# Sliding-window softmax of a hybrid decoder layer: 256 keys selected into 128 columns, parted again by GpSimd

## The chip, the cores and the metric

The kernel runs on one core of a Trainium2 chip. The metric is the device time of one execution in microseconds. The engines are TensorE (PE in the profile; PEld are its weight loads), VectorE (DVE), ScalarE (ACT), GpSimd (POOL) and SyncE (SP), which issues nearly all DMAs.

## The reference

One layer on x of 2048 tokens by 1024 channels. A projection gives the inputs of two groups of heads; group A is a gated DeltaNet (4 heads of 128), group B a sliding-window softmax (8 query heads of 64, 2 key heads). Their outputs are gated, joined, projected, added to x and normalised. The change is in group B:

```python
WINDOW = 128
BLOCK = 128
    dist = q_idx + BLOCK - s_idx                       # q_idx 0..127, s_idx 0..255
    mask = ((dist >= 0) & (dist < WINDOW))[None] & (key_pos >= 0)[:, None, :]
    s = s - slopes[:, :, None, None, None] * dist.astype(jnp.float32)
    s = jnp.where(mask, s, -jnp.inf)
    m = jnp.maximum(jnp.max(s, axis=-1), sink)
    p = jnp.exp(s - m[..., None])
    p = p / (jnp.sum(p, axis=-1, keepdims=True) + jnp.exp(sink - m)[..., None])
    o = jnp.einsum('bhgnqs,bnshd->bnqhgd', p.astype(vb.dtype), vb)
```

A block of 128 queries looks at 256 keys, its own block and the one before. The mask leaves exactly 128 of the 256 open for each query: in column j it is the key of the own block if j is at most the query's row, otherwise the key of the block before.

## The kernel before

The 2048 tokens are four units of 512; a unit has four slots, one for each pair of heads (n = 0 to 15), and a slot does one head of group A and one pair of query heads of group B over the 512 tokens. Between the steps of the heads TensorE does the dense work (the projections of the slots to come, L849, and the output projection of finished tiles, L900): `JOBS` lists it in order, each job with a begin and an end in slots, and `fill_to(n, f)` issues what is due up to the share f of slot n. `Places` holds the shares at which the steps of the heads stand. Every engine has its own program in fixed order, written out in `slot(n)`; `after(engine, counter, n, k)` makes an engine wait for a semaphore.

Group B works in two halves of 256 tokens (e = 0 and 1), each with two blocks (cc) and two heads (hd). For one half:

- TensorE `scores(n, e)` (L957) writes 256 key columns for each block and head into banks 2 and 3.
- VectorE `maxima` (L1752) adds the bias (ALiBi slope times distance, with masked keys far down), stores to `score` and takes the row maximum. ScalarE `weights` (L1353) takes the exponential with its row sum. VectorE `divide` (L1774) multiplies by the inverse of the sum.
- TensorE `turns(n, e)` (L972) transposes each 128 by 128 square of `score` into banks 2 and 3; ScalarE `copy_turned` (L1367) copies back, one bank each time.
- TensorE `values(n, e)` (L990) multiplies with `v_ring`; VectorE `gate_b` (L1782) multiplies with the gate into `y_out`, and SP spills that (`spill_b`, L668).

Between them stands group A's work: the base inverses of 16 by 16 blocks (`base_inverses`, L1793 to L1805, a chain of 30 small VectorE instructions and two closing ones, ending in `t_ready`, for which TensorE waits at L1067), further steps of the inverse (L1073 to L1095), and then the recurrence over four chunks: state product (L1107), residual (VectorE L1915), L1117, v_new (L1919), L1120, state (L1922). In the first half the transposes stand at about a quarter of the slot, ahead of the base inverses' end, and the values right before L1067; in the second half the transposes stand shortly before the recurrence and the values right before its first chunk. The convolutions (`convs`, L1582, with the small copies L1586 and L1589) are VectorE work placed between.

GpSimd subtracts the rounded part of the weights from the raw weights (`lows`, L783, four instructions for each tile): tiles of w_in in slots -1 to 2, of w_out in slots 3 and 4, and two pieces of x in slots 7 and 11. Near the end it scales and shifts output tiles 8 to 10 (L813, L817), each when VectorE has normalised it. In slot 15, SP's list is: loads of y (9 to 13), `store_tile(8)`, `load_x_tile(10)` into the buffer that tile 8 leaves, `load_y(14)`, `store_tile(9)`, and so on. VectorE's `add_half` (L1638) waits for the tile of x.

## Time and profile before

| | us |
|---|---|
| median of 3 runs | 1089.53 |
| lowest, highest | 1089.48, 1092.77 |
| the profiled execution, its own time | 1090.27 |
| its span in the trace | 1088.5 |
| VectorE busy | 688.7 |
| ScalarE busy | 532.7 |
| GpSimd busy | 115.9 |

The span runs from the first to the last instruction of the trace. Busy times of a pipelined TensorE overlap: what a group costs is better read from start to start. A row of a group gives line, engine, operation, tiles, shape and count, then busy time and mean duration, then the idle time before it. TensorE's granted clock was 0.999 of full speed.

### The profile page before, as it was taken

What the parts mean: (1) busy time and instruction counts of PE and PEld (TensorE: products, weight loads), DVE (VectorE), ACT (ScalarE), POOL (GpSimd) and SP (SyncE); (2) the same over time, 40 slices, a digit from 0 to 9 for tenths busy, and PEclk for the clock granted to TensorE, in tenths of its full rate; (3) what the DMA queues carried; (4) which work ended last, traced back from release to release, by engine and by line L of the source; (5) the groups of instructions that cost most, each with busy time, mean ns of one, the idle gap of its engine ahead of it and who ended that gap; (6) DMA issues with size and microseconds to landing.
All of it is one profiled execution on the core that took longest, in us unless ns stands there. A gap on an engine that the chain in (4) does not pass through costs nothing.

```text
span 1088.5 us, 19513 instructions
## 1 busy us (share of the span) xinstructions
PE 1064.2 (98%) x7212; PEld 846.5 (78%) x7212; DVE 688.7 (63%) x2081; ACT 532.7 (49%) x1557; POOL 115.9 (11%) x152
## 2 busy tenths in 40 slices
PE   7999999999999999999999999999999999999997
PEld 5877787778778787777887878787787878787885
DVE  5285959584665747576365665757537575758565
ACT  4557675754636454363354535435344555564300
POOL 3413132134100000020000000002000000002210
PEclk9999999999999999999999999999999999999999
DMA  8967475665553626253562551715454343622432
GB/s 282 315 209 262 163 274 195 243 208 183 201 205 109 237 73 235 87 185 98 175 228 93 165 215 46 265 49 185 132 179 157 126 157 128 215 73 63 137 116 77
DMA packets 58430, 183.55 MB, mean 169 GB/s; under 512 B 8480, under 2 KB 21216, under 8 KB 45024
## 3 DMA queue, kind: packets, MB, share of 16 engines
q1 hardware_dynamic: 58192, 182.05, 48.7%
q8 instruction: 57, 0.93, 0.3%
q10 hardware_dynamic: 144, 0.26, 0.1%
q14 instruction: 37, 0.30, 0.1%
HBM read 138.22 MB, written 44.07 MB: 167 GB/s over the span
## 4 chain that ended last, share of the span: by engine, by line
PE 65%; DVE 6%; DMA 2%; issue 1%; ACT 0%; SPq 0%; DVEq 0%
PE bank L849 33%; PE bank L900 10%; PE bank L1137 4%; PE bank L957 2%; PE bank L990 2%; PE bank L972 2%; PE bank L1107 1%; PE bank L1120 1%; PE bank L1117 1%; PE bank L1121 1%; DVE y_cols L1797 1%; DVE y_step L1793 1%; PE bank L1030 1%; PE bank L1045 1%; PE bank L1115 1%
## 5 line engine op out<-in xcount | busy, mean ns | idle before, releaser
L849 PE MATMUL bank<-xr,w 128*128 128x512 f32 x2496 | 653.9, 405 | 7.4 <-DVE xr L1534 7.4
L849 PEld LDWEIGHTS bank<-xr,w 128*128 128x128 f32 x2496 | 449.8, 189 | 101.7 <-issue 9.8
L900 PE MATMUL bank<-wo,y_split 128*128 128x512 f32 x432 | 114.4, 404 | 0.0
L900 PEld LDWEIGHTS bank<-wo,y_split 128*128 128x128 f32 x432 | 77.0, 189 | 14.6 <-issue 0.7
L1582 DVE SCALAR_TENSOR_TENSOR kq<-conv_in,convw_all,kq 128x512 f32<-128x512 f32 x96 | 77.3, 806 | 7.8 <-ACT conv_in L1191 5.8
L1487 ACT ACTIVATE o_scaled<-bank 128x128 f32<-128x128 f32 x64 | 17.7, 277 | 124.5 <-PE bank L1121 124.3
L1353 ACT ACTIVATE score<-score,neg_max 128x256 f32<-128x256 f32 (+1 forms) x128 | 62.7, 493 | 29.0 <-DVE neg_max L1759 29.0
L1919 DVE TENSOR_SCALAR steps<-bank,nb_rk 128x128 f32<-128x128 f32 x64 | 22.3, 348 | 63.9 <-PE bank L1117 63.9
L1922 DVE SCALAR_TENSOR_TENSOR state<-state,cols_all,bank 128x128 f32<-128x128 f32 x64 | 22.2, 347 | 63.2 <-PE bank L1120 63.2
L1793 DVE TENSOR_TENSOR y_step<-blocks,y_cols 128x60 f32<-128x60 f32 (+14 forms) x240 | 50.3, 210 | 12.1 <-DMA blocks<-n_spill 3.3
L783 POOL TENSOR_TENSOR xr<-y_tile,xr 128x256 fp32r<-128x256 f32 x8 | 6.0, 774 | 455.1 <-ACT xr L1172 455.1
L783 POOL TENSOR_TENSOR w<-y_tile,w 128x256 fp32r<-128x256 f32 x48 | 40.1, 866 | 101.0 <-ACT w L1180 62.5
L1797 DVE TENSOR_TENSOR y_cols<-y_step,y_cols 128x56 f32<-128x56 f32 (+6 forms) x224 | 44.4, 198 | 7.7
L1752 DVE CUSTOM_DVE_ANT_0 score<-bank,bias 128x256 f32<-128x256 f32 (+1 forms) x128 | 45.5, 411 | 6.0 <-PE bank L957 5.7
L1915 DVE SCALAR_TENSOR_TENSOR steps<-bank,cols_all,v_tok 128x128 f32<-128x128 f32 x64 | 22.1, 346 | 42.5 <-PE bank L1107 42.5
L1367 ACT ACTIVATE score<-bank 128x512 f32<-128x512 f32 (+1 forms) x64 | 33.9, 585 | 26.1 <-PE bank L972 26.1
L1137 PE MATMUL bank<-wo,xr 128*128 128x512 f32 x192 | 44.3, 390 | 0.2 <-DVE x_tile L1638 0.2
L1774 DVE TENSOR_SCALAR score<-score,denom_inv 128x256 f32<-128x256 f32 (+1 forms) x128 | 43.1, 400 | 1.1
L1137 PEld LDWEIGHTS bank<-wo,xr 128*128 128x128 f32 x192 | 35.9, 188 | 8.0 <-DVE x_tile L1638 0.6
L1446 ACT ACTIVATE blocks<-bank 128x128 f32<-128x128 f32 x16 | 4.4, 278 | 76.1 <-DVE blocks L1884 76.1
L900 PE MATMUL bank<-wo,w 128*128 128x512 f32 x144 | 38.0, 404 | 0.8 <-DVE w L1722 0.8
L1582 DVE SCALAR_TENSOR_TENSOR v_ch<-conv_in,convw_all,v_ch 128x512 f32<-128x512 f32 x48 | 37.2, 774 | 1.1
(217 smaller groups left out, 1628.3 us busy)
## 6 DMA issues: line engine op xcount, KB each, us to landing
w<-w_split SPq DMA_DIRECT2D x78, 1024.0 KB, 5.4
w_split<-w SPq DMA_DIRECT2D x26, 1024.0 KB, 5.1
blocks<-n_spill SPq DMA_DIRECT2D x32, 256.0 KB
y_spill<-y_out SPq DMA_DIRECT2D x30, 256.0 KB, 5.8
x_tile<-w_in SPq DMA_DIRECT2D x13, 512.0 KB, 6.1
y_tile<-w_in SPq DMA_DIRECT2D x12, 512.0 KB, 6.4
y_tile<-y_spill SPq DMA_DIRECT2D x12, 512.0 KB, 6.1
x_tile<-x SPq DMA_DIRECT2D x12, 512.0 KB, 3.9
```

The costliest lines, as they stand in the source:

```text
L783: ins = nc.gpsimd.tensor_tensor(dst[:, part], raw[:, part], hi[:, part], ALU.subtract)
L849: ins = nc.tensor.matmul(bank[JOBS[at].bank][:], w[:, turn % 3, wp, k, :], xr[:, xp, k], start=(step == 0), stop=(step == 3 * KT - 1))
L900: ins = nc.tensor.matmul(bank[JOBS[at].bank][:], y_place(t)[:, yp, k], wo[:, k, wp, half * UNIT:(half + 1) * UNIT], start=(step == 0), sto ...
L1137: ins = nc.tensor.matmul(bank[JOBS[at].bank][:], xr[:, yp, k, tok * P:(tok + 1) * P], wo[:, k, wp, half * UNIT:(half + 1) * UNIT], start=( ...
L1353: nc.scalar.activation(sc, sc, ACT.Exp, bias=neg_max[:, cc, hd:hd + 1], accum_out=row_sum[:, cc, hd:hd + 1]).then_inc(exp_ready.sem, 1)
L1367: nc.scalar.activation(pick(p_turned(cc)), pick(tiles(bank[2 + cc])), ACT.Copy)\
L1582: ins = nc.vector.scalar_tensor_tensor(acc, conv_in[:, c, step:step + UNIT], convw_all[:, i, c, step:step + 1], acc, ALU.mult, ALU.add)
L1752: nc.vector.tensor_tensor_reduce(out=score[:, cc, hd, 0:keys], in0=bank[2 + hd][:, cc * 256:cc * 256 + keys], in1=bias[:, hd, 2 * P - keys ...
L1774: nc.vector.tensor_scalar(p, p, denom_inv[:, cc, hd:hd + 1], None, ALU.mult).then_inc(p_scaled.sem, 1)
L1793: nc.vector.tensor_tensor(y_step[:, :, rest], blocks[:, j, :, j + 1:], y_cols[:, :, j:j + 1].to_broadcast(wide), ALU.mult).then_inc(base_s ...
L1797: nc.vector.tensor_tensor(y_cols[:, :, rest], y_step[:, :, rest], start, ALU.add).then_inc(base_step.sem, 1)
L1919: nc.vector.tensor_scalar(v_new, bank[6][:, 0:P], nb_rk[:, one], None, ALU.mult).then_inc(v_new_ready.sem, 1)
```

## The change

Before the maxima, VectorE now selects in the banks: with the mask `recent` (distance of the own block's key masked) the past key's score replaces the own one, so that 128 columns hold the 128 open keys. Maxima, exponentials and divisions work on 128 columns (`p_own`). Four squares of 128 by 128 are transposed for each half, into bank 2 alone, and one ScalarE instruction copies them into `p_past`. GpSimd then parts them with two masks: `p_past` times `tri` gives the own block's weights in `p_own`, times `past` the past block's, in place; `values` waits for each block's pair of products. The values of the second half and their gate move into the first chunk of the recurrence. On GpSimd the program becomes one list in the order of the slots, with the splits of weights and x between the parts and the scaling of tiles 8 to 10 behind the last part. On VectorE three set-up instructions are added; from slot 4 on the bias is 128 wide.

```diff
@@ block.gpsimd
+            def part(n, e):
+                if (n, e) == (0, 0):
+                    pool.wait_ge(part_masks, 1)
+                after(pool, p_copied, n, e + 1)
+                for cc in range(2):
+                    for dst, keep in ((p_own, tri), (p_past, past)):
+                        ins = nc.gpsimd.tensor_tensor(dst[:, cc], p_past[:, cc],
+                                                      keep[:].unsqueeze(1).to_broadcast([P, 2, P]), ALU.mult)
+                    ins.then_inc(p_parted.sem, 1)
...
+            turns = [turn for turn in range(TILES_W) if w_by_pool(turn)]
+            while turns[0] < 9:
+                w_low(turns.pop(0))
+            for n in range(SLOTS):
+                s, i = divmod(n, AH)
+                if n < AH - 1:
+                    w_low(turns.pop(0))
+                    part(n, 0)
+                    w_low(turns.pop(0))
+                    part(n, 1)
+                    for turn in turns[0:2]:
+                        w_low(turns.pop(0))
+                elif n == AH - 1:
+                    for ks in ((0, 1), (2, 3)):
+                        for k in ks:
+                            wo_low(k)
+                        part(n, ks[0] // 2)
+                    for k in range(4, KT - 1):
+                        wo_low(k)
+                else:
+                    if n == AH:
+                        wo_low(KT - 1)
+                    if i == AH - 1 and s < SBS - 1:
+                        x_low(s + 1, 2)
+                        x_low(s + 1, 3)
+                    part(n, 0)
+                    part(n, 1)
+            for t in POOL_TILES:
+                scale_tile(t)
@@ block.tensor
             def turns(n, e):
-                s, i = divmod(n, AH)
-                if e == 1 and i == AH - 1 and s < SBS - 1:
-                    after(pe, ba_summed, s + 1, 1)
                 for cc in range(2):
                     after(pe, p_scaled, n, 4 * e + 2 * cc + 2)
-                    if cc == 0:
-                        after(pe, p_scaled, n, 4 * e + 4)
                     for hd in range(2):
-                        for kb in range(1 if (s, e, cc) == (0, 0, 0) else 2):
-                            q = 2 * hd + kb
-                            ins = nc.tensor.transpose(bank[2 + cc][:, q * P:(q + 1) * P],
-                                                      score[:, cc, hd, kb * P:(kb + 1) * P], ident[:])
-                    ins.then_inc(p_turn_done.sem, 1)
+                        q = 2 * cc + hd
+                        ins = nc.tensor.transpose(bank[2][:, q * P:(q + 1) * P], p_own[:, cc, hd], ident[:])
+                ins.then_inc(p_turn_done.sem, 1)
...
             def values(n, e):
-                after(pe, p_turned_ready, n, 2 * e + 2)
...
-                    kbs = (0, 1) if token > 0 else (0,)
+                    kbs = (0, 1) if token > 0 else (1,)
+                    after(pe, p_parted, n, 2 * e + cc + 1)
...
-                values(n, 1)
...
                     nc.tensor.matmul(bank[6][:, 0:P], y_inv[:, c], resid, start=True, stop=True).then_inc(tr_done.sem, 1)
                     fill_to(n, at.chunk(c, 2 / 3))
+                    if c == 0:
+                        values(n, 1)
                     after(pe, v_new_ready, n, c + 1)
@@ block.scalar
             def copy_turned(n, e):
-                for cc in range(2):
-                    after(act, p_turn_done, n, 2 * e + cc + 1)
...
+                after(act, p_turn_done, n, e + 1)
+                nc.scalar.activation(p_past, bank[2][:].rearrange("p (c h n) -> p c h n", c=2, h=2), ACT.Copy)\
+                    .then_inc(p_copied.sem, 1)
@@ block.vector
+            nc.vector.tensor_scalar(past[:], tri[:], -1.0, 1.0, ALU.mult, ALU.add).then_inc(part_masks, 1)
+            nc.vector.tensor_scalar(recent[:], dist[:, P:2 * P], MASKED / 2, None, ALU.is_ge)
+            nc.vector.tensor_tensor(dist[:, 0:P], dist[:, 0:P], dist[:, P:2 * P], ALU.max).then_inc(dist_ready, 1)
...
             def maxima(n, e):
+                lead = (s, e) == (0, 0)
+                for hd in range(2):
+                    both = bank[2 + hd][:].rearrange("p (c k n) -> p c k n", c=2, k=2)[:, int(lead):]
+                    nc.vector.copy_predicated(both[:, :, 0], recent[:].unsqueeze(1).to_broadcast([P, 2 - int(lead), P]),
+                                              both[:, :, 1]).then_inc(packed.sem, 1)
+                after(dve, packed, n, 2 * e + 2)
...
                 for c in range(CH):
                     one = slice(c, c + 1)
-                    if c == 0:
-                        gate_b(n, 1)
...
                     nc.vector.scalar_tensor_tensor(state[:, i], state[:, i], col(EGT)[:, one], bank[4][:, P:2 * P],
                                                    ALU.mult, ALU.add).then_inc(state_ready.sem, 1)
+                    if c == 0:
+                        gate_b(n, 1)
```

## Rows read from the trace of the kernel before

**Rows 1.** The page: its first line and the first engine's busy time.
```profile
span 1088.5 us, 19513 instructions
...
PE 1064.2 (98%) x7212; PEld 846.5 (78%) x7212; DVE 688.7 (63%) x2081; ACT 532.7 (49%) x1557; POOL 115.9 (11%) x152
```

**Rows 2.** Waits of TensorE: who waited for whom, total us, times, longest.
```profile
PE bank L1067 <- DVE steps L1805: 3.8, 6, 1.0
```

**Rows 3.** Timeline of TensorE, slot 7: start, length, engine, line, operation, count.
```profile
485.61 1.04 PE L972 MATMUL bank<-ident,score 128*128 128x128 f32 x8
486.40 0.71 PE L900 MATMUL bank<-wo,y_split 128*128 128x512 f32 x2
```

**Rows 4.** Groups of VectorE by shape: busy us, mean ns, idle before.
```profile
L1752 DVE CUSTOM_DVE_ANT_0 score<-bank,bias 128x256 f32<-128x256 f32 x120 | 43.8, 419 | 5.9 <-PE bank L957 5.7
L1774 DVE TENSOR_SCALAR score<-score,denom_inv 128x256 f32<-128x256 f32 x120 | 41.5, 407 | 1.0
...
L1875 DVE COPY_PREDICATED r<-lower,bank 128x128 f32<-128x128 uint8 x16 | 4.8, 299 | 19.6 <-PE bank L1067 19.6
```

**Rows 5.** Timeline of GpSimd and VectorE in slot 3, beside the base inverses.
```profile
226.27 2.83 POOL L783 TENSOR_TENSOR wo<-y_tile,wo 128x256 fp32r<-128x256 f32 x4 [27.04 <-ACT wo L1186]
...
225.21 0.21 DVE L1793 TENSOR_TENSOR y_step<-blocks,y_cols 128x60 f32<-128x60 f32 x1
...
226.46 0.63 DVE L1797 TENSOR_TENSOR y_cols<-y_step,y_cols 128x52 f32<-128x52 f32 x1
...
235.93 0.31 DVE L1805 STREAM_TRANSPOSE steps<-y 128x128 f32<-128x128 f32 x1
```

**Rows 6.** Timeline of slot 5: the base inverses' first and last instruction, and L1067.
```profile
357.50 0.21 DVE L1793 TENSOR_TENSOR y_step<-blocks,y_cols 128x60 f32<-128x60 f32 x1
...
364.69 0.31 DVE L1805 STREAM_TRANSPOSE steps<-y 128x128 f32<-128x128 f32 x1
...
366.06 0.45 PE L1067 MATMUL bank<-steps,n_t 32*32 32x32 f32 x32
```

**Rows 7.** Timeline of slot 5 from the second transposes to the first chunk.
```profile
376.40 1.04 PE L972 MATMUL bank<-ident,score 128*128 128x128 f32 x8
...
379.13 1.09 PE L990 MATMUL bank<-score,v_ring 128*64 128x128 f32 x16
380.16 0.49 PE L1107 MATMUL bank<-state,kq 128*128 128x128 f32 x2
...
382.09 0.39 PE L1117 MATMUL bank<-steps,y_inv 128*128 128x128 f32 x2
...
383.71 0.38 PE L1120 MATMUL bank<-steps,k_dec 128*128 128x128 f32 x2
...
377.04 1.09 ACT L1367 ACTIVATE score<-bank 128x512 f32<-128x512 f32 x2 [1.42 <-PE bank L972]
...
377.84 2.32 DVE L1582 SCALAR_TENSOR_TENSOR v_ch<-conv_in,convw_all,v_ch 128x512 f32<-128x512 f32 x3
...
380.69 0.34 DVE L1915 SCALAR_TENSOR_TENSOR steps<-bank,cols_all,v_tok 128x128 f32<-128x128 f32 x1
```

**Rows 8.** Timeline of VectorE in slot 0: three convolution steps beside GpSimd.
```profile
66.33 3.04 DVE L1582 SCALAR_TENSOR_TENSOR kq<-conv_in,convw_all,kq 128x512 f32<-128x512 f32 x3
```

**Rows 9.** Line 1617's own instructions: duration min/median/max ns, first and last start.
```profile
L1617 DVE SCALAR_TENSOR_TENSOR pre<-pre,ea x4: 110/111/509, 31.4 to 784.1; 128x16 f32<-128x16 f32 x4
```

**Rows 10.** Timeline of slot 15: GpSimd, SP, VectorE and TensorE around output tile 8.
```profile
999.52 2.82 POOL L813 TENSOR_TENSOR x_tile<-x_tile,gain 128x256 f32<-128x256 f32 x4 [241.55 <-DVE x_tile L1662]
1002.29 2.98 POOL L817 TENSOR_TENSOR x_tile<-x_tile,shift 128x256 f32<-128x256 f32 x4
...
1008.13 0.46 SPq L658 DMA_DIRECT2D out<-x_tile  x1
...
1018.52 0.69 DVE L1638 SCALAR_TENSOR_TENSOR x_tile<-x_tile,bank 128x512 f32<-128x512 f32 x1 [0.59 <-DMA x_tile<-x]
...
1007.01 1.03 PE L972 MATMUL bank<-ident,score 128*128 128x128 f32 x8
```

More of the change, by code:

```diff
@@ L485, in build_layer @@
         denom_step = counter("denom_step", 4)
+        part_masks = sem("part_masks")
+        dist_ready = sem("dist_ready")
+        packed = counter("packed", 4)
         p_scaled = counter("p_scaled", 8)
-        p_turn_done = counter("p_turn_done", 4)
-        p_turned_ready = counter("p_turned_ready", 4)
+        p_turn_done = counter("p_turn_done", 2)
+        p_copied = counter("p_copied", 2)
+        p_parted = counter("p_parted", 4)
         pv_done = counter("pv_done", 2)
@@ L796, in w_low, with wo_low, scale_tile @@
                 lows(flat(1), raw_stage[turn % 2], flat(0)).then_inc(w_ready, 1)
-            for turn in range(TILES_W):
-                if w_by_pool(turn):
-                    w_low(turn)
-            for k in range(KT):
+            def wo_low(k):
                 pool.wait_ge(wo_high, k + 1)
                 lows(wo[:, k, 1], raw_stage[k % 2], wo[:, k, 0]).then_inc(wo_split, 1)
-            for u in (2, 3):
-                x_low(u, 2)
-                x_low(u, 3)
-            for t in POOL_TILES:
+            def part(n, e):
[7 more added lines that the diff above has]
+                    ins.then_inc(p_parted.sem, 1)
+            def scale_tile(t):
                 res = x_bufs[x_buffer(t)[0]]
@@ L881, in sum_g @@
                 after(pe, g_ready, u, 1)
-                if u > 0:
-                    after(pe, p_turned_ready, JOBS[at].n, 4)
                 g = pre[:, 5].rearrange("p h t -> p (h t)")
@@ L935, in scores @@
                     after(pe, kb_copied, s, 1)
-                    after(pe, p_turned_ready, n - 1, 4)
+                    after(pe, p_copied, n - 1, 2)
                     if i == 0:
@@ L940, in scores @@
                 else:
-                    after(pe, p_turned_ready, n, 2)
+                    after(pe, p_copied, n, 1)
                 for cc in range(2):
@@ L1034, in slot @@
                     after(pe, vb_copied, s, 1)
-                    after(pe, p_turned_ready, n - 1, 4)
+                    after(pe, p_copied, n - 1, 2)
                     for c in range(CH):
@@ L1347, in weights @@
                 for cc in parts:
-                    keys = n_keys(n // AH, 2 * e + cc)
                     if cc == 0:
@@ L1351, in weights @@
                     for hd in range(2):
-                        sc = score[:, cc, hd, 0:keys]
+                        sc = p_own[:, cc, hd]
                         nc.scalar.activation(sc, sc, ACT.Exp, bias=neg_max[:, cc, hd:hd + 1],
@@ L1563, in slopes @@
             def slopes(n):
+                width = 2 * P if n < AH else P
                 for hd in range(2):
-                    nc.vector.tensor_scalar(bias[:, hd], dist[:], pair_all[:, n % AH, SLOPE, hd:hd + 1], None, ALU.mult)\
+                    nc.vector.tensor_scalar(bias[:, hd, 0:width], dist[:, 0:width], pair_all[:, n % AH, SLOPE, hd:hd + 1], None, ALU.mult)\
                         .then_inc(bias_ready.sem, 1)
+            dve.wait_ge(dist_ready, 1)
             slopes(0)
@@ L1748, in maxima @@
                     after(dve, pv_done, n, 1)
+                lead = (s, e) == (0, 0)
[4 more added lines that the diff above has]
+                after(dve, packed, n, 2 * e + 2)
                 for cc in range(2):
-                    keys = n_keys(s, 2 * e + cc)
+                    first = P if lead and cc == 0 else 0
                     for hd in range(2):
-                        nc.vector.tensor_tensor_reduce(out=score[:, cc, hd, 0:keys],
-                                                       in0=bank[2 + hd][:, cc * 256:cc * 256 + keys],
-                                                       in1=bias[:, hd, 2 * P - keys:], scale=BD ** -0.5, scalar=LOWEST,
+                        nc.vector.tensor_tensor_reduce(out=p_own[:, cc, hd],
+                                                       in0=bank[2 + hd][:, cc * 256:cc * 256 + P],
+                                                       in1=bias[:, hd, first:first + P], scale=BD ** -0.5, scalar=LOWEST,
                                                        op0=ALU.add, op1=ALU.max, accum_out=row_max[:, cc, hd:hd + 1])\
```

22 lines of the change are left out of this document (8 added, 14 removed).

## The prediction

> **What bounds the kernel now.** I read the page first: TensorE is busy for 1064.2 of the 1088.5 us span [rows 1]. The engine's waits come next: behind the start, the largest is 3.8 us in 6 waits at L1067, for the end of VectorE's base inverses (L1805) [rows 2]. So the time is the sum of what TensorE is given, and any new wait of more than a few tenths of a microsecond is paid in full. The profiled execution took 1090.27 us, 1.77 more than its span and 0.74 more than the median of the runs; the sum below is made against 1090.27 and 0.74 is taken off at the end.
>
> **Fewer transposes.** 248 transposes become 128. Eight of them took 0.79 us from their first start to the start of the matmul behind them [rows 3], 0.1 us each (the 273 ns that one lasts overlaps its neighbour). 120 x 0.1 = 12.0 us less for TensorE, 0.4 us in each of the 32 half slots (0.2 in the first).
>
> **VectorE and ScalarE.** A maximum over 256 keys took 419 ns and a division 407 ns (mean) [rows 4]; both go to 128. The added selection (256 elements, bank to bank) has no row; the nearest is the 128-element copy_predicated at 299 ns [rows 4]. Bounds: 0.3 us (as that one) to 0.9 us (twice it and some) for each; I take 0.4. Two are added per half slot, 0.8 us and 0.1 for the wait behind them, against 4 x 0.13 from the maxima and 4 x 0.03 from the divisions: +0.25 us in VectorE's chain. In slots 3 to 15 it is hidden, since VectorE waits there for TensorE's transposes or inverse steps; in slots 0 to 2 the second half is VectorE's chain down to the division, so 3 x 0.2 = +0.6 us (without cover in all slots it would be 32 x 0.25 = 8). One eviction of 512 columns replaces two, the exponentials halve, the bias is half as wide from slot 4 on: nothing waits for them. The three set-up instructions stand in VectorE's slack before slot 0: nothing.
>
> **GpSimd, first halves.** Each half slot now has four GpSimd products of 256 elements. The same kind on that engine is 2.83 us for four [rows 5], so 3.0 us with the wake-up: 95 us more for an engine that was busy for a tenth of the span. Values of the first half are due about 8 us after the copy, so they do not wait. What pays is VectorE. In slot 3 eight such instructions (the four shown and four more 3.9 us later) ran beside the base inverses; the chain took 235.93 + 0.31 - 225.21 = 11.03 us [rows 5]. With none beside it, it took 364.69 + 0.31 - 357.50 = 7.50 us [rows 6]. That is 3.53 / 8 = 0.44 us for each GpSimd instruction: one small VectorE instruction is held at 0.63 instead of 0.21 us until it ends [rows 5]. The new products follow the first transposes, which is where this chain runs: four fall into it in nearly every slot, +1.76 us.
> - Slots 0, 1, 2, 3, 7 and 11 have no slack at L1067 (TensorE waits there already; in 0 to 2, 7 and 11 the products queue behind a split and still land in the chain): 6 x 1.75 = 10.5, and 0.9 in slot 3, where the next split of w_out slides into the longer chain. 11.4 us.
> - Slots 5, 6, 9 and 10: the chain ended at 365.00 and TensorE came at 366.06 [rows 6], slack 1.06. 1.76 - 1.06 = +0.7 us; four times, 2.8 us.
> - The others, read in the same way: 0 in 4 and 12 (the chain starts late there, on a DMA), -0.4 in 8, +0.3 in 13 and 14, +0.9 in 15. 1.1 us.
> First halves: +15.3 us, the saving of 0.4 included.
>
> **GpSimd, second halves.** The second values move behind the first trial residual. In slot 5 the transposes started at 376.40, the copy at 377.04, and k_dec x v_new (L1120) at 383.71 [rows 7]. GpSimd would run from 377.7 to about 382, values are wanted at about 382.3: hardly a direct wait. But VectorE is then in the convolution of v (377.84, three steps of 0.75) and two small copies, and its residual (L1915) started at 380.69 [rows 7]. Three steps beside GpSimd took 3.04 instead of 2.32 us [rows 8]: +0.7. The copies have no row beside GpSimd. Bounds: nothing, and 1.1 us for both (held to the end of a product each). The nearest row, a small instruction with two SBUF inputs, went from 111 to 509 ns [rows 9]; I take 0.3 each, 0.6. The gate's 0.4 us have moved away, so the residual is ready 0.9 us later than now, at 381.9. TensorE comes for it 1.4 us earlier (0.4 of transposes gone, and the values, 379.13 to 380.16, not yet issued), waits, and issues L1117 at 382.0, where it stood at 382.09; the 1.0 us of values, which hid VectorE's work before, now come after it. L1120 is 0.9 us later than before instead of 0.4 earlier. By slots: 4, 5, 8 and 9 +0.9 each (3.6); 6 and 10, where the residual addition of an output tile stands in the same place and L1117 waits already, +1.9 each (3.8); 12 to 14, with half the filling, +1.0 each (3.0); 0 to 2 +0.9 each and the 0.2 above (3.3); 3, where the second part queues behind a split of w_out, +0.6; 7 and 11, where VectorE is idle, -0.4 each. Second halves: +13.5 us.
>
> The copies stand alone in one point: by the Trainium skill, VectorE: DVE Perf Modes, section "Mode 2x_2P", fp32 copies in SBUF use both read ports, and by GPSIMD Engine Reference, section "Key points", such instructions contend with GpSimd. By that rule both copies would be held like the rest; no row of the kernel before shows it for them.
>
> **GpSimd's order at the end.** The scaling of output tile 8 (2.82 + 2.98 us, at 999.5) ran before the last second half; now it is written behind part(15, 1). It can start only after the transposes (1007.01), 1.3 us for transposing and copying and 3.0 us of products, and takes 5.8: the store of tile 8, issued at 1008.13, is issued about 9 us later. The load of tile 10 waits for that store, and VectorE added tile 10 at 1018.52, ahead of the residual of chunk 1 and after a short wait for just this load [rows 10]. So VectorE, then TensorE, stand still: +9.1, less 0.6 because the divisions of slot 15 no longer meet the scaling: +8.5 us. SP's other entries behind it (load_y(14), store of tile 9) have their use 7 us or more after that and shift with it. In slots 3, 7 and 11 spill_b leaves 5 us later and the copy of vb waits for it on ScalarE; its bank is needed only for bq, 2 us after: nothing.
>
> **Sum.** 15.3 + 13.5 + 8.5 = +37.3 us. 1090.27 + 37.3 - 0.74 = 1126.8, given as 1127 us.
>
> **Rivals.**
> - Copies held in full (by the rule above): each second half except in 3, 7, 11 and 15 another 0.5 later, 12 x 0.5 = 6: 1133 us. For it: every kind of small VectorE instruction that reads two SBUF inputs was held. Against: this kind has no row. 0.20.
> - Copies not held: the residual is 0.6 us earlier in the same 12 slots, 7 us less: 1120 us. 0.20.
> - The end is covered: the store or the load of tile 10 takes less than its 10.4 us, or the addition is late anyway: without the 8.5 us, 1118 us. Against: the short wait at 1018.5. 0.10.
> - Faster, the other side: products in place with a broadcast mask do not hold the base inverses. The place is L1067, the price 0.44 us for each GpSimd instruction; below about 0.1 us the slack of slots 4 to 15 covers it and the transposes win. Then 1089.5 - 12 + 8.5 = 1086 us, and 1077.5 if the end is covered as well. For it: nothing but that the operands differ. 0.12.
> - The change does nothing that can be measured (0.3%, 3.3 us, is about what a measurement of this kernel can tell): the holds come to some 12 us by chance. 0.03.
> The forecast itself has 0.35. The range 1102 to 1138 takes in the forecast, both bounds of the copies, a covered end with free copies (1111), first halves a third cheaper beside that (1105), and a selection of 0.9 us each in slots 0 to 2 (+3); about 0.15 lies outside. Faster 0.12, same 0.03, slower 0.85.
>
> **What the profile after would show.** TensorE's busy time near 1052 and more idle; the wait L1067 <- L1805 at 15 us or more instead of 3.8; base inverses of 9.2 us with four held instructions of 0.65; L1117 waiting for L1915 in most slots; a still TensorE of 8 us near the end, behind the load of x_tile; selections of 0.4 us. If L1067's wait is unchanged while GpSimd works beside the chain, the forecast is wrong at its main term.

## The result and the profile after

The changed kernel takes 1126.57 us (median of 4 runs, 1125.51 to 1128.42), the kernel before 1090.94 beside it: a ratio of 1.0328, with a 95% interval of 1.0301 to 1.0354. The profiled execution took 1125.51 us, its span is 1123.5. The forecast was 1127 us. The sum was made against 1089.53 us, the median of the kernel before at that time: +37.3 forecast, +35.6 measured beside it.

The first lines of its page (span; busy time of each engine; granted clock of TensorE in 40 slices):

```profile
span 1123.5 us, 19402 instructions
...
PE 1068.9 (95%) x7092; PEld 842.9 (75%) x7092; DVE 722.8 (64%) x2148; ACT 503.7 (45%) x1525; POOL 219.6 (20%) x280
...
PEclk9999998998999999999999999999999999999899
```

Against [rows 1], TensorE has 120 instructions fewer and is still busy 4.7 us longer, where the forecast wanted about 1052 us: something stretched its instructions. The row of the clock, which the forecast did not reckon with, has slices below 9. The largest waits of TensorE behind the start (who waited for whom, total us, times, longest):

```profile
PE bank L1095 <- DVE steps L1839: 25.2, 14, 4.2
...
PE bank L1144 <- DVE steps L1947: 11.8, 13, 5.4
```

L1095 and L1839 are L1067 and L1805 of [rows 2]: 3.8 us became 25.2. L1144 waits for the residual (L1947, L1915 before). The new and the halved operations of VectorE (groups by shape: busy us, mean ns, idle before):

```profile
L1808 DVE TENSOR_SCALAR score<-score,denom_inv 128x128 f32<-128x128 f32 x128 | 33.6, 325 | 1.1
L1786 DVE CUSTOM_DVE_ANT_0 score<-bank,bias 128x128 f32<-128x128 f32 x128 | 29.6, 287 | 1.1
L1780 DVE COPY_PREDICATED bank<-recent,bank 128x256 f32<-128x256 uint8 x56 | 21.2, 424 | 7.9 <-PE bank L992 7.7
```

A selection costs 0.42 us (0.4 taken), a maximum is 0.13 us cheaper than in [rows 4], a division 0.08.

**Where the 35.1 us are.** I cut each slot at TensorE's own marks and summed the differences to the kernel before over the 16 slots; each number is the difference of the same stretch in two traces, and a row adds up, but for rounding, to the difference of the spans. The sections are: what lies ahead of slot 0; A, from the start of a slot to L1067/L1095 (the first half: transposes, base inverses); B, from there to the second transposes; C, from those to k_dec x v_new of chunk 0 (residual and second values); D, the rest of the slot. All kernels are told of below. Each row is one profiled execution, which need not be the median one: f2_none_back's took 1089.21 us where its median is 1084.52.

| kernel | ahead | A | B | C | D | sum |
|---|---|---|---|---|---|---|
| changed | 0.8 | 13.4 | 8.0 | 3.7 | 9.2 | 35.1 |
| e1_order | 0.8 | 13.5 | 12.1 | 3.7 | 2.8 | 32.9 |
| e2_no_first | 0.5 | -2.9 | -0.4 | 6.2 | 10.6 | 14.0 |
| e3_no_second | 1.1 | 14.6 | 8.9 | -3.0 | 3.0 | 24.6 |
| e4_fill | 0.7 | 14.5 | 1.1 | 6.8 | 9.5 | 32.6 |
| f1_none | 0.8 | -4.4 | 0.4 | -1.8 | 2.3 | -2.7 |
| f2_none_back | 1.3 | -0.2 | 2.0 | -6.7 | 2.4 | -1.2 |
| f3_select | 0.8 | -2.3 | 1.6 | -1.1 | 3.3 | 2.4 |
| f4_half | 1.0 | 3.4 | 3.3 | 5.4 | 1.7 | 14.7 |
| g1_own_select_back | 0.0 | -0.5 | 0.6 | -0.3 | 1.8 | 1.5 |
| g2_late_wo | 1.4 | -3.7 | -1.0 | -1.8 | 0.2 | -4.9 |
| g3_vector_back | 0.6 | 5.7 | 0.7 | 35.3 | 0.2 | 42.5 |
| g4_select_back | 0.0 | -1.4 | 1.4 | 17.9 | 1.1 | 19.0 |

**The first half, slot 5.** Timelines (start, length, engine, line, count; in brackets the idle time before it): VectorE's first base-inverse steps and last, then TensorE in slot 3.

```profile
374.01 0.76 DVE L1827 TENSOR_TENSOR y_step<-blocks,y_cols 128x60 f32<-128x60 f32 x1
374.80 0.66 DVE L1831 TENSOR_TENSOR y_cols<-y_step,ident 128x60 f32<-128x60 f32 x1
375.50 0.66 DVE L1827 TENSOR_TENSOR y_step<-blocks,y_cols 128x56 f32<-128x56 f32 x1
376.19 0.66 DVE L1831 TENSOR_TENSOR y_cols<-y_step,y_cols 128x56 f32<-128x56 f32 x1
376.88 0.21 DVE L1827 TENSOR_TENSOR y_step<-blocks,y_cols 128x52 f32<-128x52 f32 x1
...
383.08 0.31 DVE L1839 STREAM_TRANSPOSE steps<-y 128x128 f32<-128x128 f32 x1
```

```profile
252.59 0.65 PE L1095 MATMUL bank<-steps,n_t 32*32 32x32 f32 x32 [4.21 <-DVE steps L1839]
253.17 2.08 PE L992 MATMUL bank<-k_ring,q_in 64*128 64x256 f32 x8
255.18 2.50 PE L886 MATMUL bank<-xr,w 128*128 128x512 f32 x5
```

Four products, four held instructions of 0.66 to 0.76 us; the chain takes 383.39 - 374.01 = 9.38 us against 7.50 in [rows 6]. This is the forecast's step as it stands: 1.9 us for four products (1.76 forecast). In slot 3 TensorE waits 4.21 us for the chain, and behind that wait it is slow: its 32 small matmuls take 0.65 us (0.45 in [rows 6]).

**The clock.** TensorE's granted clock in stretches behind the wait at L1095, in slots 0, 2, 3, 5 and 7, and in slot 15 behind a stall (us from : to, length, busy TensorE and instructions, granted clock, DMA share, GB/s):

```profile
80.50:84.00 3.50, 3.50 (x43) 0.58 0.02 5
...
190.70:197.50 6.80, 6.80 (x81) 0.53 0.01 2
252.60:259.40 6.80, 6.80 (x82) 0.56 0.11 41
383.40:390.00 6.60, 6.55 (x105) 1.00 0.78 293
518.40:525.00 6.60, 6.60 (x105) 1.00 0.43 133
...
1049.00:1056.00 7.00, 3.32 (x9) 0.60 0.74 243
```

After waits of 2.80, 2.80 and 4.21 us (slots 0, 2 and 3) the granted clock is at its lower level, 1.2 of 2.4 GHz, for nearly the whole stretch; after 0.59 us (slot 5) and 1.98 us (slot 7) it stays at 2.4. The same fall stands behind the waits of slots 1 and 11 (2.65 and 2.35 us). B is longer by 1.28, 1.23, 2.47 and 2.53 us in slots 0 to 3 and by 1.54 in 11, and shorter by 1.07 in slot 15, where the divisions no longer meet the scaling of tile 8.

**The second half, slot 5.** All engines' timeline, answering to [rows 7]:

```profile
393.79 0.60 PE L1001 MATMUL bank<-ident,score 128*128 128x128 f32 x4
...
394.83 3.03 DVE L1610 SCALAR_TENSOR_TENSOR v_ch<-conv_in,convw_all,v_ch 128x512 f32<-128x512 f32 x3
...
395.10 1.07 POOL L810 TENSOR_TENSOR score<-score,tri 128x256 f32<-128x256 f32 x1 [18.33 <-ACT score L1390]
...
397.27 1.17 POOL L810 TENSOR_TENSOR score<-score,tri 128x256 f32<-128x256 f32 x1
...
397.78 0.15 DVE L1614 COPY tails<-conv_in 128x9 f32<-128x9 f32 x1
...
397.97 0.16 DVE L1617 COPY conv_in<-tails 128x9 f32<-128x9 f32 x1
398.05 0.35 DVE L1947 SCALAR_TENSOR_TENSOR steps<-bank,cols_all,v_tok 128x128 f32<-128x128 f32 x1
...
398.46 0.49 PE L1144 MATMUL bank<-steps,y_inv 128*128 128x128 f32 x2 [0.28 <-DVE steps L1947]
```

The three convolution steps take 3.03 us, as forecast, and the products beside them 1.07 to 1.17 where 0.74 is usual: both are longer while they run together. But the two small copies run in the middle of the product that lasts from 397.27 to 398.44 and take 0.15 and 0.16 us, as ever. The residual starts 4.26 us behind the second transposes; the forecast had it at 5.5.

**The end.** TensorE's stall in slot 15, from the timeline:

```profile
1044.68 0.35 SPq L660 DMA_DIRECT2D out<-x_tile  x1
...
1047.32 0.35 SPq L652 DMA_DIRECT2D x_tile<-x  x1
...
1050.96 0.69 DVE L1666 SCALAR_TENSOR_TENSOR x_tile<-x_tile,bank 128x512 f32<-128x512 f32 x1 [5.23 <-DMA x_tile<-x]
...
1052.68 0.80 PE L1144 MATMUL bank<-steps,y_inv 128*128 128x128 f32 x2 [5.39 <-DVE steps L1947]
```

The store of tile 8 goes out late, the load of tile 10 waits for it, VectorE for the load and TensorE for VectorE, as laid out in the prediction: from the first k_dec x v_new to the last, the slot is 7.35 us longer than before, for 8.5 forecast.

### The profile page after: what moved, and what is told of

Read it like the earlier page. It is cut to its first block and busy times, and to the rows that moved or that the text cites. A ratio compares the mean times of both kernels' runs of the same rounds, so it can differ in the third digit from the quotient of the medians.

```text
span 1123.5 us, 19402 instructions
## 1 busy us (share of the span) xinstructions
PE 1068.9 (95%) x7092; PEld 842.9 (75%) x7092; DVE 722.8 (64%) x2148; ACT 503.7 (45%) x1525; POOL 219.6 (20%) x280
## 5 line engine op out<-in xcount | busy, mean ns | idle before, releaser
L886 PE MATMUL bank<-xr,w 128*128 128x512 f32 x2496 | 660.6, 408 | 7.6 <-DVE xr L1557 7.5
L810 POOL TENSOR_TENSOR score<-score,tri 128x256 f32<-128x256 f32 x64 | 56.1, 877 | 567.0 <-ACT score L1390 567.0
L935 PEld LDWEIGHTS bank<-wo,y_split 128*128 128x128 f32 x432 | 77.0, 189 | 14.6 <-issue 0.7
L1827 DVE TENSOR_TENSOR y_step<-blocks,y_cols 128x60 f32<-128x60 f32 (+14 forms) x240 | 64.9, 270 | 12.5 <-DMA blocks<-n_spill 3.7
L1381 ACT ACTIVATE score<-score,neg_max 128x128 f32<-128x128 f32 x128 | 49.9, 392 | 33.0 <-DVE neg_max L1793 33.0
L1831 DVE TENSOR_TENSOR y_cols<-y_step,y_cols 128x56 f32<-128x56 f32 (+6 forms) x224 | 56.3, 251 | 7.7
L810 POOL TENSOR_TENSOR score<-score,past 128x256 f32<-128x256 f32 x64 | 53.2, 831 | 0.0
L1947 DVE SCALAR_TENSOR_TENSOR steps<-bank,cols_all,v_tok 128x128 f32<-128x128 f32 x64 | 22.2, 346 | 47.9 <-PE bank L1134 47.9
L1610 DVE SCALAR_TENSOR_TENSOR v_ch<-conv_in,convw_all,v_ch 128x512 f32<-128x512 f32 x48 | 44.4, 925 | 1.1
L1144 PE MATMUL bank<-steps,y_inv 128*128 128x128 f32 x128 | 26.4, 288 | 11.8 <-DVE steps L1947 11.8
L992 PE MATMUL bank<-k_ring,q_in 64*128 64x256 f32 (+1 forms) x240 | 37.0, 428 | 0.0
```

Of the source, the lines that this page charges most:

```text
L810: ins = nc.gpsimd.tensor_tensor(dst[:, cc], p_past[:, cc], keep[:].unsqueeze(1).to_broadcast([P, 2, P]), ALU.mult)
L886: ins = nc.tensor.matmul(bank[JOBS[at].bank][:], w[:, turn % 3, wp, k, :], xr[:, xp, k], start=(step == 0), stop=(step == 3 * KT - 1))
L935: ins = nc.tensor.matmul(bank[JOBS[at].bank][:], y_place(t)[:, yp, k], wo[:, k, wp, half * UNIT:(half + 1) * UNIT], start=(step == 0), sto ...
L992: ins = nc.tensor.matmul(to[:, 0:width], q, k_ring[rows, first % 8 * P:first % 8 * P + width], start=True, stop=True)
L1144: nc.tensor.matmul(bank[6][:, 0:P], y_inv[:, c], resid, start=True, stop=True).then_inc(tr_done.sem, 1)
L1381: nc.scalar.activation(sc, sc, ACT.Exp, bias=neg_max[:, cc, hd:hd + 1], accum_out=row_sum[:, cc, hd:hd + 1]).then_inc(exp_ready.sem, 1)
```

## The experiments

The theory after the result: VectorE's base inverses and convolution steps are held by GpSimd's products; behind the long waits that this gives TensorE its clock falls as well; the end is a matter of order. The rivals: the other parts of the change (selections, place of the values, set-up) carry the loss; the slow clock costs nothing of its own; any GpSimd work would do the same. The kernels of a letter ran beside the kernel before, which took 1091.24 us (e), 1091.63 (f) and 1091.37 (g).

**e1_order.** One edit in GpSimd's order, slot 15:

```diff
                     part(n, 0)
+                    if n == SLOTS - 1:
+                        scale_tile(POOL_TILES[0])
                     part(n, 1)
```

> The changed kernel with the scaling of output tile 8 put back ahead of the last pair of products on GpSimd. The forecast's third term (GpSimd's order at the end, +8.5 us): the recurrence of slot 15 loses its stall at L1144 (7.4 us between the first and the last L1149 of the slot), while the divisions of slot 15 meet the scaling again (up to 1 us): 1119 us, 1117 to 1121. Rival, the end is covered or bound by another transfer: within 2 us of the changed kernel, 1125 or more.

Measured: 1122.37 us (1121.48 to 1123.25, two executions), 4.2 less, where 1117 to 1121 was expected. The stall is gone (from the first k_dec x v_new to the last, slot 15 is 0.2 us longer than before, not 7.35), so the mechanism stands, but in this execution the clock fell in slots 7 and 12 too (0.74 and 0.73 granted over 6.6 and 6.3 us, behind waits of 2.43 and 2.02 us; in the first trace those waits were 1.98 and 1.80 us and it held). B is 4.1 us longer, 2.9 of them in these two slots and 1.2 in slot 15, where the divisions meet the scaling again. What an avoided stall gives is read from its slot, not from the total.

**e2_no_first** and **e3_no_second.** The parting is left out in one half; the values read the whole copy twice there.

```diff
             def part(n, e):
+                if e == 0:      # e3: e == 1
+                    return
...
-                    after(pe, p_parted, n, 2 * e + cc + 1)
+                    after(pe, p_copied, n, 1)   # in that half; e3: n, 2
```

> The changed kernel without GpSimd's four products in the first halves; the values of the first halves read the unparted copy, so the parting of these is left out of the computation. Theory, the products hold the base inverses: the chain takes 7.5 us again in the slots with nothing else on GpSimd, the wait at L1095 falls from 25 us to 5 or less, TensorE's clock stays at its upper level in slots 0 to 3 and 11, and the time is 30 us less: 1097 us, 1093 to 1101. Rival, VectorE is late by its own new selection: the wait stays above 15 us and the time above 1115.

> The changed kernel without the four products in the second halves (their values read the unparted copy: that parting is left out); nothing is in front of the scaling of tile 8 then either. Theory, the products hold the convolution of v ahead of the first residual: L1144 no longer waits for L1947 in slots 4 to 14, 8 us, and the stall of slot 15 is gone, 8 us: 1110 us, 1107 to 1114. Rival, moving the values behind the residual costs by itself: only the 8 us of the end are won, 1118 or more.

Measured: 1106.68 us (1104.53 to 1108.82) and 1113.55 us (1112.03 to 1115.08), two executions each. Without the first products A falls by 16.3 us and B by 8.4: the base inverses last as before in all slots but 3 (13.19 us, 11.03 before) and 14 (8.16), and the clock falls nowhere in slots 0 to 3 or 11, though slot 3 still has a wait of 2.71 us; it falls in slot 12. 20 us came back where I expected 30. A and B together gave 24.7, not 30; C took 2.5 of them back, since TensorE now comes earlier to the residual and waits for VectorE, and D 1.4. The wait for the base inverses is 7.8 us in all, above the 5 expected. Without the second products C falls by 6.7 us and the end's stall goes as well (D -6.2, because tile 8 is scaled at once): 13.0 us.

**e4_fill.** TensorE is given idle work ahead of the long waits, into a bank free at that time.

```diff
                 values(n, 0)
+                for _ in range({3: 5}.get(n, 3) if n < AH or n == 11 else 0):
+                    nc.tensor.matmul(bank[3][:], ident[:], k_dec[:].rearrange("p t n -> p (t n)"), start=True, stop=True)
                 after(pe, t_ready, n, 1)
```

> The changed kernel with idle work for TensorE in front of the wait at L1095: three multiplications of 512 columns in slots 0, 1, 2 and 11 and five in slot 3, shorter than the wait there, their result unused. Theory, after the long waits TensorE is granted its lower clock and the stretch from L1095 to the second transposes is longer by 1.2 to 2.5 us in these five slots: the clock stays at its upper level there and the time falls by 8 to 9 us, to 1118, 1116 to 1120, though TensorE is given 10 us more to do. Rival, those stretches are longer because VectorE's chain is: nothing is won, 1125 or more.

The granted clock behind the same waits in slots 0, 1, 2 and 3:

```profile
80.40:84.00 3.60, 3.58 (x79) 1.00 0.02 5
134.90:138.30 3.40, 3.40 (x79) 1.00 0.02 5
189.30:196.00 6.70, 6.70 (x121) 1.00 0.03 12
249.90:256.70 6.80, 6.80 (x120) 1.00 0.07 27
```

Measured: 1122.18 us (1121.34 to 1123.01, two executions), 4.4 less although VectorE's chain is as long as in the changed kernel. So the slow clock has a cost of its own. It is half of the 8 to 9 us expected, for two reasons that the trace shows. B gives back 10 us in the five slots, but the clock now falls in slots 7 and 12, behind waits of 1.98 and 1.68 us, and takes 3.1 of them; and 3.1 more are lost in C of slots 0 to 2, where TensorE, now early, waits for the residual.

**f1_none** and **f2_none_back.** No parting at all (the values read the whole copy twice); in the second the values and their gate also stand where they did before.

```diff
             def part(n, e):
+                return
...
-                    after(pe, p_parted, n, 2 * e + cc + 1)
+                    after(pe, p_copied, n, e + 1)
...
+                values(n, 1)              # f2 only, ahead of the chunks
                 for c in range(CH):
                     fill_to(n, at.chunk(c))
...
-                    if c == 0:
-                        values(n, 1)      # f2 only; gate_b(n, 1) likewise
```

> Leaves the parting out in both halves (the values read the unparted copy twice, so the attention output is not the reference's); everything else as in the changed kernel. Theory (the parting's products are the whole loss, and the two halves add): 1126.6 less the 20 us that leaving out the first halves' products gave and the 13 us of the second halves': 1093 (1090 to 1096), and TensorE's clock falls in none of slots 0 to 3. Rival (select, later values and fuller slots cost by themselves, and the two halves' products share one cost): 1100 or more.

> As f1_none, and the second values and their gate go back to their place of before, ahead of the first state step. Theory: the values' 1.2 us per slot after the residual are 0.15 us dearer than the 1.05 us they took ahead of the step, so 16 slots give back 2.4 us: 1.5 to 4 us under f1_none, which is under before. Rival (ahead of the step the gate delays the residual by about as much): within 1 us of f1_none.

Measured: 1090.19 us (1087.55 to 1095.05), ratio 0.9989 (0.9972 to 1.0006), and 1084.52 us (1079.16 to 1092.37), ratio 0.9941 (0.9914 to 0.9967). The first is what the theory wants in its total: without GpSimd's products nothing of the 3.3% is left. It also shows that free parting would have won nothing that can be measured in the changed kernel's order.

One expectation failed: the clock does fall in slot 3 of f1_none (B +1.4 there). Its timeline has no product, but three groups of w_out's splits beside the base inverses where [rows 5] has two:

```profile
226.74 0.21 DVE L1828 TENSOR_TENSOR y_step<-blocks,y_cols 128x60 f32<-128x60 f32 x1
...
236.66 2.76 POOL L785 TENSOR_TENSOR wo<-y_tile,wo 128x256 fp32r<-128x256 f32 x4 [2.61 <-ACT wo L1216]
...
236.76 0.65 DVE L1832 TENSOR_TENSOR y_cols<-y_step,y_cols 128x8 f32<-128x8 f32 x1
...
239.60 0.31 DVE L1840 STREAM_TRANSPOSE steps<-y 128x128 f32<-128x128 f32 x1
```

The chain takes 13.17 us there with no product beside it, 11.03 before and 14.93 in the changed kernel. So 2.1 of slot 3's 3.8 us belong to the splits of w_out and to when they run, not to the products.

f2_none_back is 5.7 us under f1_none, more than the 1.5 to 4 that I expected. The executions of f2_none_back scatter more (1079 to 1092 against 1088 to 1095), and the traced one, in which the clock fell in slots 3, 7 and 12, is not the faster of the two; the cause is read from C, which is 4.9 us shorter. There the values ahead of the step cover VectorE's way to the residual, for which f1_none waits 0.45 us in each of slots 0 to 2 and 0.89 in 6 and 10.

**f3_select.** Each product becomes a select by an affine condition (query column at or beyond key partition, and its complement), with e1_order's edit.

```diff
-                        ins = nc.gpsimd.tensor_tensor(dst[:, cc], p_past[:, cc],
-                                                      keep[:].unsqueeze(1).to_broadcast([P, 2, P]), ALU.mult)
+                        ins = nc.gpsimd.affine_select(dst[:, cc], p_past[:, cc], [[0, 2], [sign, P]], ALU.is_ge, 0.0,
+                                                      base=min(sign, 0), channel_multiplier=-sign)
```

> The changed kernel with tile 8's scaling ahead of the last parting, and each GpSimd product replaced by a select by an affine condition, with one input and no mask tile; the output is the reference's. Theory (only GpSimd operations with two SBUF inputs hold VectorE's): the base inverses keep 7.5 to 8.5 us and the time is that of f1_none or a few us above, 1092 to 1098. Rival 1 (any GpSimd operation in SBUF holds them): 1122 as with the products, as far as one select lasts as long as one product. Rival 2 (no hold, but a select lasts several times a product and the values wait for it): above 1125.

Measured: 1093.21 us (1089.52 to 1095.26), ratio 1.0008 (0.9993 to 1.0024). GpSimd's group, and VectorE's first steps of slot 5 beside four selects:

```profile
L810 POOL TENSOR_SCALAR_AFFINE_SELECT score<-score 128x256 f32<-128x256 f32 x128 | 63.8, 532 | 561.7 <-ACT score L1392 561.7
```

```profile
362.55 0.42 DVE L1829 TENSOR_TENSOR y_step<-blocks,y_cols 128x60 f32<-128x60 f32 x1
363.01 0.32 DVE L1833 TENSOR_TENSOR y_cols<-y_step,ident 128x60 f32<-128x60 f32 x1
363.37 0.32 DVE L1829 TENSOR_TENSOR y_step<-blocks,y_cols 128x56 f32<-128x56 f32 x1
363.72 0.32 DVE L1833 TENSOR_TENSOR y_cols<-y_step,y_cols 128x56 f32<-128x56 f32 x1
364.08 0.21 DVE L1829 TENSOR_TENSOR y_step<-blocks,y_cols 128x52 f32<-128x52 f32 x1
```

The same elements move through the same memory, and a VectorE instruction is held by about 0.11 us (0.32 for 0.21; 0.21 in the first) in place of 0.45: base inverses of 8.03 us, between 7.50 and 9.38. "Any GpSimd work holds alike" is ruled out. But the theory as I had put it, that only GpSimd operations with two SBUF inputs hold VectorE, is not borne out either, since a select with one input still does. A select is also shorter than a product (0.41 for 0.73 us by itself), and no run keeps the length and takes away the second input alone: which of the two makes the hold smaller is open.

**f4_half.** Half the products, same output: the past block's values take the whole copy, the own block's take P * tri with the difference of the two blocks' values, which VectorE makes once per unit of 512 tokens (called superblock in the expectation; with e1_order's edit).

```diff
-                    for dst, keep in ((p_own, tri), (p_past, past)):
-                        ins = nc.gpsimd.tensor_tensor(dst[:, cc], p_past[:, cc], ...)
+                    ins = nc.gpsimd.tensor_tensor(p_own[:, cc], p_past[:, cc],
+                                                  tri[:].unsqueeze(1).to_broadcast([P, 2, P]), ALU.mult)
...
+                    nc.vector.tensor_tensor(v_ring[:, 5 + low:9], v_ring[:, 1 + low:5], v_ring[:, low:4],
+                                            ALU.subtract).then_inc(vdiff_ready.sem, 1)
```

> Half the dose, same output: tile 8's scaling ahead of the last parting, and GpSimd makes only the own block's product; the past block's values take the whole copy, and the own block's take the difference of the two blocks' values, one subtraction of 512 columns per superblock on VectorE. Theory (the hold goes by the number of products): base inverses 0.95 us longer than before in place of 1.9, no fall of TensorE's clock in slots 0 and 1, 1122 less 8 in the first halves, 6 by the clock, 3 in the second halves: 1105 (1101 to 1110). Rival (the hold is per stretch in which GpSimd works at all): base inverses 1.5 us longer or more and 1116 or above.

Measured: 1103.90 us (1102.52 to 1105.05), inside the expected 1101 to 1110. Base inverses of slot 5: 8.49 us, 0.99 more than before, 0.5 for each product. The hold goes by the number of products.

**g1_own_select_back** and **g2_late_wo.** f4_half with a select for its product and the values back ahead of the step; the second also keeps the third group of w_out's lower parts off slot 3's base inverses.

```diff
-                        ins = nc.gpsimd.tensor_tensor(p_own[:, cc], p_past[:, cc], ...)
+                        ins = nc.gpsimd.affine_select(p_own[:, cc], p_past[:, cc], [[0, 2], [1, P]], ALU.is_ge, 0.0,
+                                                      base=0, channel_multiplier=-1)
...
                         for k in ks:
+                            if k == 2:                        # g2 only
+                                after(pool, t_ready, n, 1)
                             wo_low(k)
```

> The version that the runs point to, same output as the reference's: one select of the own block per chunk on GpSimd (two per half in place of four products), the past block's values from the whole copy and the own block's from the difference of the two blocks' values, tile 8's scaling ahead of the last parting, and the second values and their gate back ahead of the first state step. Theory (what is left is a hold of 0.13 us per select and a short wait ahead of the values): f2_none_back's 1084.5, 1.5 for the hold in slots 0 to 3, 7 and 11, 1.5 for the wait, 1.5 for the subtraction in slots 0 and 12: 1089 (1086 to 1092). Rival (the values so early wait out transposes, copy and selects in every slot, 0.5 us or more each): 1095 and slower than before.

> As g1_own_select_back, and in slot 3 the third group of wo's lower parts waits until the base inverses are done. Theory (that group's four products beside slot 3's base inverses cost 0.46 us each): 1.8 us under g1_own_select_back. Rival (the later split of wo is waited for by ScalarE or TensorE): the same time or more.

Measured: 1089.96 us (1086.65 to 1091.76), ratio 0.9981 (0.9967 to 0.9996), and 1086.68 us (1083.49 to 1090.16), ratio 0.9952 (0.9930 to 0.9975). Both have the reference's output. The second is 4.7 us, 0.5%, under the kernel before beside it, with the whole interval below 1. Its gain over the first is 3.3 us (1.8 expected). In the two traces, whose spans differ by 6.5, slot 3 is 5.1 us shorter up to its first k_dec x v_new: base inverses of 11.47 in place of 13.41 us, and no fall of the clock behind them.

**g4_select_back** and **g3_vector_back.** f3_select with the values back ahead of the step; and g1_own_select_back with the product on VectorE, out of the bank, the second one behind the convolution steps.

```diff
+                values(n, 1)                  # both, ahead of the chunks
...
+                part(n, 0)                    # g3 only: on VectorE
                 base_inverses(n)
...
                 after_jobs(n, at.step0)
+                part(n, 1)                    # g3 only
```

> As f3_select (four selects per half, no difference of values), with the second values and their gate back ahead of the first state step. Theory (the place of the values cost 5.7 us with no parting; ahead of the step they wait some tenths for four selects): 1093.2 less 5.7, 2 to 3 for the wait: 1090 (1087 to 1093). Rival (the wait for four selects eats the place's gain): 1093 or more.

> As g1_own_select_back, but VectorE makes the own block's product itself, 512 columns out of the bank behind ScalarE's copy, ahead of the base inverses and ahead of the gate; GpSimd parts nothing. Theory (VectorE has no slack ahead of the base inverses in slots 0 to 3, 7, 11 and 12 and some elsewhere): f2_none_back's 1084.5, 7 times 0.7, 1.5 for the subtraction and 0.2 per slot ahead of the values: 1094 (1090 to 1099). Rival (VectorE waits enough to take it everywhere): 1087 to 1090, no slower than g1_own_select_back.

Measured: 1110.11 us (1106.57 to 1113.08) and 1131.25 us (1127.79 to 1132.76). Both expectations are far off, in the same place. The largest waits of TensorE in g4_select_back, and in g3_vector_back:

```profile
PE bank L1020 <- POOL score L810: 15.5, 25, 2.6
```

```profile
PE bank L1024 <- DVE score L1820: 27.6, 13, 3.4
```

Ahead of the step TensorE comes to the values 1.7 us behind the transposes (slot 0 of g4_select_back). Two selects nearly fit in (g1_own_select_back has four such waits, 2.8 us in all), four don't, and a product that stands behind VectorE's convolution steps does so least. I had priced the wait at tenths because I counted from the copy and not from the last thing in the queue ahead of the parting.

The waits are not the whole of it. The values of slot 0 of g4_select_back, and the granted clock of the stretch behind them:

```profile
90.97 0.66 PE L1020 MATMUL bank<-score,v_ring 128*64 128x128 f32 x8 [0.99 <-POOL score L810]
92.05 0.66 PE L1020 MATMUL bank<-score,v_ring 128*64 128x128 f32 x8 [0.42 <-POOL score L810]
```

```profile
92.60:96.40 3.80, 3.80 (x15) 0.55 0.52 199
```

Behind two waits of 0.99 and 0.42 us the clock fell; the same in slots 1 and 2, which with slot 3 give 12.6 of the 17.9 us of C. In g3_vector_back the clock fell inside C in slots 0, 1, 2, 5, 6, 8, 10 and 12. How much of C is wait and how much clock was not tried apart. This also answers why the change moved the values: with four GpSimd operations per half they have to stand later, and the move costs 5.7 us.

## Why the prediction was right, and where it was not

- **Transposes, -12.0 us: right.** With all parting gone, the stretch from the first transposes to L1095 is 0.41 to 0.46 us shorter in slots 4 to 10 and 13 of f1_none, and f2_none_back's stretch from the second transposes to the first state step 0.37 to 0.46 us in every slot.
- **VectorE's chain, +0.6 us: small, wrong sign.** The selection is 0.42 us (0.4 taken), a maximum is cheaper by the 0.13 taken, a division by 0.08, where 0.03 was taken without a row. But in slots 0 to 2 section B is 0.3 us shorter in f1_none and f2_none_back. The step left out what the halved exponentials and bias give back there; that it is those was not tried by itself.
- **First halves, +15.3 us: right, 13.4 measured (A).** 1.9 us per four products against 1.76; slots 5, 6, 9 and 10 came to +0.6 (0.7). Slot 3 gave 3.8, more than its 2.65: f1_none shows that the slide of w_out's splits costs 2.1 there, not 0.9. Slot 4 gave -2.5 for 0: two waits up to its transposes (0.83 us for ScalarE, 0.96 for the divisions) are gone, which I had not looked for; that the later split of w_out removed them was not tried.
- **Second halves, +13.5 us: right in direction, too large by 8.5.** C came to 3.7 us and D outside slot 15 to 1.3, 5.0 in all. Two things are in this. First, the step "0.3 us for each small copy" failed, together with VectorE's start there: the copies were not held at all (0.15 and 0.16 us beside a product), and VectorE reached the convolution of v 1.04 us behind the transposes, not 1.44. The convolution steps' +0.7 was right. Second, in slots 0 to 2 the fallen clock brought TensorE late to the residual, so that little of VectorE's lateness was left to wait for: C gave 0.8 us there, and 3.9 in e4_fill, where the clock was kept up (3.3 forecast). By the Trainium skill (VectorE: DVE Perf Modes, section "Mode 2x_2P") a copy uses both ports only if the outermost dimension is even, or odd and the same on both sides; these copies go from 3 rows of 3 to a run of 9, or back, and do not meet that. The prediction had left the condition out, so "by that rule both copies would be held" misread the page. The trace agrees with the page: 12 and 11 of them ran beside a product, all within 10 ns of those that did not.
- **The end, +8.5 us: right, 7.35 measured**, and e1_order and e3_no_second take it away by two ways.
- **What was missing: the clock.** B grew by 8.0 us where nothing was forecast. e4_fill shows that 4.4 us of the total hang on it, net of two new falls and of C. The forecast valued a new wait at its length; some waits also cost what follows them. The length of the wait alone does not tell which: the clock fell behind 2.35 us and not behind 1.98 in the changed kernel, but behind 1.68 in e4_fill, and in slot 3, at 2.71 us both times, it fell in f1_none and not in e2_no_first.
- **The sum.** That 1127 met 1126.6 is luck. In the traces, against +37.3: ahead of slot 0 +0.8 for nothing, first halves 13.4 for 15.3, second halves 5.0 for 13.5, B 8.0 for nothing, slot 15's D 7.9 for 8.5. The two large errors cancel, and they are not independent: about 3 us of the second halves went missing because of the clock. Without its fall this would have been close to the rival of the copies not held (1120); e4_fill's 1122.2, in which it fell in two other slots, is the nearest run. The rival in which the products hold nothing put its bound at 0.1 us per GpSimd instruction. f3_select, with 0.11 to 0.13 and the end mended, is at 1093, and f1_none, with no parting at all, at 1090, not at 1077: the saving of the transposes alone does not make the change faster, because the later place of the values takes 5.7 us of it and slot 3's splits, with the clock behind them, another 3.5 in f1_none's trace. The rest of the gap was not traced to a cause.

## What to carry to other kernels

An operation that is moved to an idle engine is paid on the engine whose memory accesses it meets; price it as (number of instructions) x (hold of one short instruction there), and look whether another instruction of the same engine does the same work with one operand less. Look also at what else of that engine's list comes to stand elsewhere: here a third group of weight splits came to lie on the same chain, with the products and without them. Where an operation can be made smaller by algebra (one mask and a difference of values in place of two masks), that pays twice: in the hold, and in the latency that decides how early its user may stand. When TensorE is the bound, a long wait can be dearer than its length, and an avoided stall may be lost again at the next producer; sum by sections of the slot before trusting a total that comes out right.

## What the runs showed of the hardware that I had not expected

- Beside a GpSimd product of 128x256, short VectorE instructions with two SBUF inputs went from 0.21 to 0.66 us, and the convolution's 512 columns from 0.75 to 1.10; copies of 9 columns (0.15, 0.16 us) kept their time, and so did two selections in the bank (0.42 and 0.43) and a maximum with one operand in a bank (0.29) that met a GpSimd subtraction. Not only two inputs are held: the 14 divisions in SBUF that met subtractions took 0.50 to 0.78 us instead of 0.28. The product itself went from 0.73 to 1.17 us beside convolution steps.
- A GpSimd select over the same 128x256 elements took 0.41 us by itself where a product took 0.73, and held a VectorE instruction by 0.11 us where the product held it by 0.45.
- The granted clock fell to its lower level behind TensorE waits of 2.35 to 4.21 us in the changed kernel, and not behind 0.59 and 1.98. In e1_order it also fell behind 2.43 and 2.02 us, for 1.5 and 1.4 us of delay, in f4_half behind 1.77 in slot 2 and not behind 1.72 and 1.75 in slots 0 and 1, and in g4_select_back behind two waits of 0.99 and 0.42. So a small change in a wait can be worth several times as much, and which wait is followed by a fall could not be told from its length in these runs.
- What was not tried: the kernel before with the third group of w_out's lower parts held back as in g2_late_wo. Its slot 3 had eight held instructions, so part of g2_late_wo's gain may be open to it too. Nor was the changed kernel run with its splits of w_out alone put back.
